# Layer 1 of a two-layer generator: four modulation rows summed on VectorE, and attention's maxima taken one unit ahead

## The chip, the cores and the metric

The kernel runs on one core of one Trainium2 chip. The metric is the device time of one execution in microseconds. The time before is 958.49 us, the median of three runs (957.53 to 961.4). All data are fp32; PE is TensorE, DVE VectorE, ACT ScalarE, POOL GpSimd, SP the engine whose queue issues the weight loads.

## The reference, cut to what matters

Two layers act on 256 latent tokens and 256 context tokens of width 1024. Each layer has a mixer and a mixture of 32 experts, each behind a norm and a modulation by a vector of the sample. Layer 1's mixer is an attention with two kinds of heads.

```python
mod_l = (silu(c) @ mod_w[i] + mod_b[i]).reshape(b, 6, 1, d)      # six rows of 1024 per layer
hl = modulate(rms_norm(xl, norm_g[i, 0]), mod_l[:, 0], mod_l[:, 1])
# layer 1: q, k, v from hl @ w_in, normed by head, rotated (rope) for latent tokens
s = einsum(q, k) * scale ; p = softmax(s) ; o = p @ v
o_m = attend(q_m, k_m, v_m, MLA_SCALE)                             # 4 heads
o_d = rms_norm(attend(q1, k1, v_d) - lam * attend(q2, k2, v_d), g_sub) * (1 - lam_init)   # 4 heads, two maps each
xl = xl + mod_l[:, 2] * (concat(o_m, o_d) @ w_out)
h2 = modulate(rms_norm(xl, norm_g[i, 1]), mod_l[:, 3], mod_l[:, 4])
xl = xl + mod_l[:, 5] * moe(h2)                                    # 32 experts in 8 groups, top 2 of one group
```

Layer 1 gives no context output, so rows 2 to 5 of its modulation are needed for the latent stream alone.

## The kernel before, in words

Every engine has its own program, and semaphores tie them. The order of work is written out by hand.

**Weights.** `stream_plan` lists all weight units in the order of their use, mostly 2 MB each. SP's loop (L970) issues them in that order, and each issue waits until the unit's slot is free. `slot_plan` (L154 on) gives the slots: a ring of 7, and for the experts four more places lent by other tensors (WORK_SLOT, X_SLOT, B_SLOT, PART_SLOT). WORK_SLOT of layer 1 waits for the 16th turned attention output, X_SLOT for the saved x and the routing's logits, PART_SLOT for the stored h2 rows. `freed` says which semaphore frees a unit: a modulation unit is freed by PE's multiplication of that row.

**Modulation.** A row of the modulation is 1024 x 1024 weights in two units. `mod_multiply(i)` runs 32 PE records with 32-column weights of the activated conditioning vectors (`mod_part`, L1029), ScalarE copies the bank (`mod_copy`, L1497), `mod_turn` turns it by four small matmuls (L1051), VectorE adds the bias (`mod_columns`, L1855). Rows 8 and 9 (row 2 and 3 of layer 1) are done during the projection, row 8 behind item 16 and row 9 behind the last item; rows 10 and 11 are cut into eight parts, one behind each of the units 8 to 15 of attention (`mod_in_attention`).

**Projection** (`project_pe`, the item loops of `attention_scalar` and `attention_vector`). 28 items of one tile of tokens each: 0 to 5 ckv and ql, 6 to 15 the 512-wide kd, qd and vd (11 and 13 to 15 are vd, without norm), 16 to 23 kvm, 24 to 27 qm. For each, PE multiplies (L473, L483, L486), ScalarE squares (L641, L638), VectorE sums the squares (`sums`, L1719), GpSimd takes the power -1/2 (L2203, L2204), VectorE scales the rows (`rows_of`, L1744, L1748, L1754) and rotates those of latent tokens (L1700 to L1706), PE turns them two items later (L504), ScalarE copies the columns.

**Attention.** 16 units: 0 to 7 are MLA heads, scored in pairs (L532, L535), 8 to 15 differential heads with two maps (L541). PE's step i holds scores(i), values(i-2) (L561), turn_o(i-3) (L571), a modulation part, and probs(i-1), the transposes of the probabilities (L550). ScalarE's step holds the squares of the output (L671), exps(i) (L656), o_cols(i-3) (L664) and the copy of the turned probabilities (L677). VectorE's step holds maxima(i) (L1791, L1793), output_rows(i-2) (L1819) and normalize(i) (L1800 to L1805). Bank 5 holds one unit's values at a time, so values(i) wait for output_rows(i-1). Afterwards come `project_out` (L1133), the norm and routing of the experts, and the experts (L1255, L1280).

Of the kernel before, what the change touches and what calls it, by code (L numbers as in the profile page):

```python
# [20 lines left out]
P = 128  # L21
D = 1024
# [131 lines left out]
def slot_plan(stream):  # L154
# [35 lines left out]

OIN = {"ckv": (768, 960), "ql": (0, 256), "kd": (960, 1472), "qd": (256, 768), "vd": (1472, 1984)}


def generator_kernel(nc, a, out):
# [4 lines left out]
    with ExitStack() as ctx:  # L199
# [135 lines left out]
        MOD_ITEM = 16  # L335
        MOD_BANK = (6, 6, 6, 6, 6, 6, 7, 6, 6, 6, 7, 7)
# [118 lines left out]
        def project_pe(pe, loaded, mod_multiply, mod_turn):  # L455
# [63 lines left out]
        def attention_pe(pe, mod_turn, mod_in_attention, gates):  # L519
# [44 lines left out]
            def turn_o(i):  # L564
                pe.wait_ge(sem("o_rows"), i + 1)
                if i:
                    pe.wait_ge(sem("o_cols"), i)
                else:

                    pe.wait_ge(sem("mod_rows"), 10)  # L570
                pe.transpose(bank[6][:, 0:P], OR[i % 2], ident).then_inc(sem("o_turned"), 1)  # L571

            for i in range(n_units + 3):
# [6 lines left out]
                if i == 2:  # L580
                    mod_turn(9)
                if 8 <= i < 16:
                    mod_in_attention(i - 8)
                if 0 <= i - 1 < n_units:
                    probs(i - 1)
                if i == n_units:
                    pe.wait_ge(sem("exp_done"), n_units - 1)
                    gates("a1", 1, 2, (1,), (0, 1))
                elif i == n_units + 1:
                    mod_turn(10)  # L590

        def attention_scalar(act, mod_copy, gate_rows):
# [26 lines left out]
            for i, (kind, t, p) in enumerate(ITEMS):  # L619
                if i == MOD_ITEM + 1:  # L620
                    mod_copy(8)
# [25 lines left out]
            mod_copy(9)  # L647
# [18 lines left out]
            def o_squares(i):  # L666
# [4 lines left out]
                act.activation(OR[j], bank[5][:, 0:P], ACT.Square, accum_out=oss[:, j:j + 1]).then_inc(sem("o_squares"), 1)  # L671
# [7 lines left out]
            for i in range(n_units + 3):  # L679
                if 0 <= i - 2 < n_units and UNITS[i - 2][0]:  # L680
                    o_squares(i - 2)
                if i == 12:
                    mod_copy(10)
# [6 lines left out]
                if i == n_units:  # L690
                    mod_copy(11)
                elif i == n_units + 1:
# [304 lines left out]
        def _(pe):  # L997
# [34 lines left out]
            def mod_in_attention(j):  # L1032

                i, part = 10 + j // 4, j % 4
                if part % 2 == 0:
                    loaded(pe, where[("mod",) + MOD_PAIRS[i] + (part // 2,)])
                if part == 0:
                    pe.wait_ge(sem("mod_cols"), 10)
                    pe.wait_ge(sem("mod_rows"), i)
                mm = mod_part(i, MOD_BANK[i], (2 * part, 2 * part + 1))  # L1040
                if part == 3:
                    mm.then_inc(sem("mod_mm"), 1)

            def mod_turn(i):

                pe.wait_ge(sem("mod_rows"), 12 if i >= 10 else i + 1)
# [7 lines left out]
            def mod(i):  # L1054
                mod_multiply(i)
                mod_turn(i)

# [78 lines left out]
            def route(L):  # L1136
# [61 lines left out]
                pe.wait_ge(sem("mod_cols"), (7, 12)[L])  # L1198
# [254 lines left out]
            project_pe(pe, loaded, mod_multiply, mod_turn)  # L1453
            attention_pe(pe, mod_turn, mod_in_attention, gates)
            mod_turn(11)
# [3 lines left out]
            pe.wait_ge(sem("mod_cols"), 12)  # L1459
# [8 lines left out]
        def _(act):  # L1468
# [203 lines left out]
            attention_scalar(act, mod_copy, gate_rows)  # L1672
# [700 lines left out]
```

## Time and profile before

| | us |
|---|---|
| median of 3 runs | 958.49 (957.53 to 961.4) |
| span of the profiled execution | 954.8 |
| PE busy | 851.6 (89%) |
| DVE busy | 323.4 (34%) |
| ACT busy | 170.0 (18%) |
| POOL busy | 170.5 (18%) |
| HBM read | 293.66 MB, 321 GB/s over the span |

The profile gives the profiled execution by its span, from the first to the last instruction; a time of its own around that isn't shown. The stages by the clock of the span: layer 0 to about 480 us, the norm of layer 1's mixer to 497, projection to 617.8, attention to 688.2, output projection to 715.8, norm and routing to about 731, experts to the end. Busy time of an engine is the sum of its instructions; a busy PE isn't a PE at its peak. The granted clock is 1.00 at 2.4 GHz and 0.50 at 1.2 GHz.

### The profile page before, as it was taken

What the parts mean: (1) busy time and instruction counts of PE and PEld (TensorE: products, weight loads), DVE (VectorE), ACT (ScalarE), POOL (GpSimd) and SP (SyncE); (2) the same over time, 40 slices, a digit from 0 to 9 for tenths busy, and PEclk for the clock granted to TensorE, in tenths of its full rate; (3) what the DMA queues carried; (4) which work ended last, traced back from release to release, by engine and by line L of the source; (5) the groups of instructions that cost most, each with busy time, mean ns of one, the idle gap of its engine ahead of it and who ended that gap; (6) DMA issues with size and microseconds to landing.
All of it is one profiled execution on the core that took longest, in us unless ns stands there. A gap on an engine that the chain in (4) does not pass through costs nothing.

```text
span 954.8 us, 10284 instructions
## 1 busy us (share of the span) xinstructions
PE 851.6 (89%) x3887; PEld 376.0 (39%) x3887; DVE 323.4 (34%) x711; ACT 170.0 (18%) x419; POOL 170.5 (18%) x210
## 2 busy tenths in 40 slices
PE   4899999999999999868769999888899999779786
PEld 2444445447333333223257443354546333223222
DVE  1279997217111211111132441636405111011011
ACT  2301022115000000000042112445414000000000
POOL 2100391221220222220212211300110111011001
PEclk9899999999999999889969999999999999889898
DMA  9999454709999999999989024372657999999994
GB/s 362 408 414 388 152 211 186 300 35 324 328 407 405 372 400 375 420 400 417 374 361 387 1 100 165 135 307 107 281 230 265 381 406 409 418 418 425 413 418 180
DMA packets 33975, 298.00 MB, mean 312 GB/s; under 512 B 6560, under 2 KB 6866, under 8 KB 16252
## 3 DMA queue, kind: packets, MB, share of 16 engines
q1 hardware_dynamic: 26928, 283.26, 73.5%
q0 software_dynamic: 6912, 13.92, 4.1%
q8 instruction: 39, 0.64, 0.3%
q14 instruction: 20, 0.16, 0.1%
q10 hardware_dynamic: 76, 0.02, 0.0%
HBM read 293.66 MB, written 12.58 MB: 321 GB/s over the span
## 4 chain that ended last, share of the span: by engine, by line
PE 50%; DMA 21%; DVE 15%; issue 6%; ACT 3%; SPq 3%; PEld 2%; POOL 0%; another core or an unknown queue 0%; PEldq 0%; POOLq 0%; DVEq 0%
PE bank L1255 14%; DVE WORK L2156 9%; PE bank L473 9%; PE bank L1280 7%; DMA ring<-in_gu_pack 5%; PE bank L1405 5%; DMA B<-in_gu_pack 5%; DMA WORK<-in_gu_pack 4%; DMA ring<-in_win_pack 3%; PE bank L1133 3%; SPq L970 2%; PE bank L1352 2%; DVE small L1791 1%; PE bank L1029 1%; DMA h_rows<-B 1%
## 5 line engine op out<-in xcount | busy, mean ns | idle before, releaser
L1255 PE MATMUL bank<-ring,hT 128*64 128x512 f32 x688 | 210.5, 633 | 23.4 <-DMA ring<-in_gu_pack 16.6
L2070 DVE SCALAR_TENSOR_TENSOR hT<-hT,WORK,bank 128x256 f32<-128x256 f32 x34 | 16.3, 480 | 327.3 <-ACT hT L1556 327.3
L1255 PEld LDWEIGHTS bank<-ring,hT 128*64 128x64 f32 x688 | 62.1, 145 | 117.9 <-issue 117.7
L2156 DVE SCALAR_TENSOR_TENSOR WORK<-WORK,par 128x512 f32<-128x512 f32 x116 | 90.7, 861 | 0.0
L473 PE MATMUL bank<-ring,hT 128*128 128x512 f32 (+2 forms) x256 | 88.0, 499 | 0.7 <-ACT hT L1519 0.7
L1280 PE MATMUL bank<-ring,WORK 128*64 128x512 f32 x368 | 83.5, 595 | 1.6 <-ACT WORK L1561 1.6
L1255 PE MATMUL bank<-WORK,hT 128*64 128x512 f32 x128 | 59.8, 609 | 9.1 <-issue 7.6
L1561 ACT ACTIVATE WORK<-bank 128x256 f32<-128x256 f32 x34 | 13.1, 384 | 281.9 <-PE bank L1264 281.9
L1352 PE MATMUL bank<-hT,ring 128*128 128x512 f32 x128 | 58.4, 616 | 2.2 <-DMA ring<-in_win_pack 2.2
L473 PEld LDWEIGHTS bank<-ring,hT 128*128 128x128 f32 x256 | 46.0, 190 | 35.8 <-issue 34.0
L1029 PE MATMUL bank<-ring,cs 128*32 128x512 f32 x384 | 49.2, 638 | 9.5 <-DMA ring<-in_mod_pack 7.4
L1255 PE MATMUL bank<-X,hT 128*64 128x512 f32 x112 | 53.9, 629 | 4.0 <-DMA B<-in_gu_pack 2.7
L1405 PE MATMUL bank<-ring,B 128*128 128x512 f32 x128 | 56.6, 596 | 0.8 <-DVE B L2173 0.8
L852 POOL DMA_INDIRECT hT<-h_rows,smalli x21 | 20.0, 954 | 170.8 <-PE bank L1229 87.8
L2203 POOL TENSOR_SCALAR small<-small 128x1 f32<-128x1 f32 (+2 forms) x46 | 11.4, 247 | 209.7 <-ACT WORK L671 66.3
L1255 PE MATMUL bank<-B,hT 128*64 128x512 f32 x96 | 45.3, 617 | 1.3 <-issue 1.3
L1280 PEld LDWEIGHTS bank<-ring,WORK 128*64 128x64 f32 x368 | 25.7, 137 | 48.2 <-issue 44.7
L1352 PEld LDWEIGHTS bank<-hT,ring 128*128 128x128 f32 x128 | 24.9, 198 | 34.2 <-issue 30.9
L1405 PEld LDWEIGHTS bank<-ring,B 128*128 128x128 f32 x128 | 23.8, 190 | 31.2 <-issue 27.7
L865 POOL DMA_INDIRECT latents<-WORK,smalli x8 | 8.2, 1029 | 153.4 <-DVE WORK L2088 130.5
L2204 POOL TENSOR_TENSOR small<-small,cst 128x1 f32<-128x1 f32 (+2 forms) x46 | 33.8, 734 | 3.8
L1556 ACT ACTIVATE hT<-bank 128x256 f32<-128x256 f32 x34 | 13.1, 384 | 118.6 <-PE bank L1255 114.7
(297 smaller groups left out, 1039.1 us busy)
## 6 DMA issues: line engine op xcount, KB each, us to landing
ring<-in_gu_pack SPq DMA_DIRECT2D x38, 2048.0 KB, 22.3
ring<-in_mod_pack SPq DMA_DIRECT2D x24, 2048.0 KB, 12.8
ring<-in_down_pack SPq DMA_DIRECT2D x20, 2048.0 KB, 26.7
WORK<-in_gu_pack SPq DMA_DIRECT2D x6, 2048.0 KB, 32.7
ring<-in_wout_pack SPq DMA_DIRECT2D x4, 2048.0 KB, 15.7
ring<-in_gu_pack SPq DMA_DIRECT2D x8, 1024.0 KB, 28.0
ring<-in_win_pack SPq DMA_DIRECT2D x3, 2048.0 KB, 36.8
X<-in_gu_pack SPq DMA_DIRECT2D x3, 2048.0 KB, 30.3
```

The source lines that it names most:

```text
L473: mm = pe.matmul(dst[:, 0:hi - lo], hT[:, k, t * P:(t + 1) * P], w[:, k, :], start=k == 0, stop=k == KC - 1)
L852: return pool.indirect_dma_start(XG[s], None, h2d[:, :], bass.IndirectOffsetOnAxis(ap=smalli[0:ST, i:i + 1], axis=0), bounds_check=rows_ - ...
L970: sp.dma_start(dst, src).then_inc(sem(f"weights_in{at}"), 16)
L1029: mm = pe.matmul(bank[b][at:at + 32, :], cs[:, k, :], w, start=k < 2, stop=k >= KC - 2)
L1133: mm = pe.matmul(bank[OUT_BANKS[L][i % 2]][:, :], lhs(k, j), w[:, k, :], start=k == 0, stop=k == KC - 1)
L1255: mm = pe.matmul(dst[ST * x:ST * x + ST, :], HG[L][s][:, k, :], columns(units[x], 512 * k, 512), start=k == 0, stop=k == KC - 1)
L1280: mm = pe.matmul(bank[5 + s][ST * h:ST * h + ST, :], HET[s][:, f, ST * x:ST * x + ST], columns(n, 2048 * x + 1024 * f + 512 * h, 512), sta ...
L1352: mm = pe.matmul(b[:, :], w[:, k, 256 * part + P * (m % 2):256 * part + P * (m % 2) + P], hT[:, k, :], start=k == 0, stop=k == KC - 1)
L1405: mm = pe.matmul(bank[OUT_BANKS[0][i % 3]][:, :], mixT[:, (k + 4) % KC, j * P:(j + 1) * P], w[:, (k + 4) % KC, :], start=k == 0, stop=k == ...
L2070: dve.scalar_tensor_tensor(out=T1[L][s], in0=SG[L][s], scalar=cwt[:, at:at + 1], in1=src[:, 0:DE], op0=ALU.mult, op1=ALU.mult).then_inc(se ...
L2156: ins = dve.scalar_tensor_tensor(out=acc, in0=src, scalar=w, in1=acc, op0=ALU.mult, op1=ALU.add)
L2204: pool.tensor_tensor(dst, dst, C("half", 0, 1).to_broadcast([P, n]), ALU.pow).then_inc(sem(name), 1)
```

## The change

It has two parts. First, rows 2 to 5 of layer 1's modulation are no longer multiplied on PE. VectorE accumulates, for the latent stream alone, weight rows times the conditioning value of each partition, over the eight chunks of the contraction, in 64 instructions of 128x512. They stand behind the items 6 to 15 of its projection program in the numbers of `SUM_STEPS`. PE then sums over the partitions: `sum_rows` for row 2 (as a row broadcast to all partitions), `sum_columns` for rows 3 to 5 (as columns). GpSimd clears the accumulator of row 2 and loads its bias. A modulation unit is freed by VectorE's count, and the order in which free slots are given is sorted by `LATER`. Second, in attention the maxima of unit i+1 are taken before unit i is normalised, and the first map of a differential unit isn't scaled: the second is weighed by lambda and the ratio of the sums, and 1/sum goes into the output rows and their squares. The cut diff (`gates`, `mod_copy`, `mod_turn` calls of these rows go away throughout):

```diff
 def slot_plan(stream):
+    where_second = stream.index(("lora",))
+    def order(at):
+        u = stream[held[at]]
+        if u in early:
+            return 0, early.index(u)
+        if u in LATER:
+            return 2, LATER.index(u)
+        return 1, held[at]
     for n, u in enumerate(stream):
         expert = u[0] in ("gu", "down")
+        if n > where_second and (not expert or WORK_SLOT not in free):
+            free.sort(key=order)
...
+LATER = [("mod", 1, 1, 0), ("mod", 1, 1, 1), ("oin", "ckv"), ("oin", "ql"), ("mod", 1, 2, 0), ("mod", 1, 2, 1), ("oin", "qd"),
+         ("mod", 1, 3, 0), ("mod", 1, 3, 1), ("oin", "kd"), ("mod", 1, 4, 0), ("mod", 1, 4, 1), ("mod", 1, 5, 0), ("oin", "vd"), ("mod", 1, 5, 1),
+         ("lora",), ("wout", 1, 0), ("wout", 1, 1)]
...
+        SUMMED = [(1, 2), (1, 3), (1, 4), (1, 5)]
+        SUMS = [[MR[:, h, :] for h in (0, 1)], [B[:, 2048 + 512 * h:2560 + 512 * h] for h in (0, 1)],
+                [B[:, 3072 + 512 * h:3584 + 512 * h] for h in (0, 1)], [GB[:, 0, 512 * h:512 * h + 512] for h in (0, 1)]]
+        SUM_STEPS = {6: 4, 7: 4, 8: 8, 9: 5, 10: 5, 11: 10, 12: 5, 13: 8, 14: 8, 15: 7}
         def freed(n):
             u = STREAM[n]
+            if u[0] == "mod" and u[1:3] in SUMMED:
+                return "sum_done", 4 * TAPS + 2 * KC * SUMMED.index(u[1:3]) + KC * (u[3] + 1)
...
         def project_pe(...):
             for i in range(len(ITEMS) + 2):
                 if i < len(ITEMS):
                     source(i)
-                if i == MOD_ITEM:
-                    mod_multiply(8)
-                elif i == MOD_ITEM + 4:
-                    mod_turn(8)
-                elif i == len(ITEMS):
-                    mod_multiply(9)
+                if i == len(ITEMS):
+                    sum_columns()
                 if i >= 2:
                     turn(i - 2)
         def attention_pe(...):
             for i in range(n_units + 3):
...
-                if i == 2:
-                    mod_turn(9)
-                if 8 <= i < 16:
-                    mod_in_attention(i - 8)
                 if 0 <= i - 1 < n_units:
                     probs(i - 1)
                 if i == n_units:
                     pe.wait_ge(sem("exp_done"), n_units - 1)
-                    gates("a1", 1, 2, (1,), (0, 1))
+                    sum_rows()
...
+            def sum_columns():
+                pe.wait_ge(sem("mod_cols"), 8)
+                for j in (1, 2, 3):
+                    pe.wait_ge(sem("sum_done"), 4 * TAPS + 2 * KC * (j + 1))
+                    for k in range(KC):
+                        mm = pe.matmul(bank[7][:, 16 * j + 2 * k:16 * j + 2 * k + 2], SUMS[j][k // 4][:, P * (k % 4):P * (k % 4) + P],
+                                       C("ones").to_broadcast([P, 2]), start=True, stop=True)
+                mm.then_inc(sem("mod_turned"), 1)
+            def sum_rows():
+                pe.wait_ge(sem("sum_done"), 4 * TAPS + 2 * KC)
+                for h in range(2):
+                    pe.matmul(bank[h][:, :], C("ones").to_broadcast([P, P]), SUMS[0][h], start=True, stop=True).then_inc(sem("gate_mms"), 1)
...
         def attention_vector(...):
+            def mod_sum(n):
+                j, k, h = n // (2 * KC), n // 2 % KC, n % 2
+                unit = where[("mod",) + SUMMED[j] + (k // 4,)]
+                if n == 0:
+                    dve.wait_ge(sem("brow_in"), 80)
+                if n % KC == 0:
+                    loaded(dve, unit)
+                if n >= 2:
+                    dve.wait_ge(sem("sum_done"), 4 * TAPS + n - 1)
+                w, c, acc = columns(unit, 1024 * (k % 4) + 512 * h, 512), cs[:, k, 1:2], SUMS[j][h]
+                if k == 0 and j:
+                    ins = ts(acc, w, c, None, ALU.mult)
+                else:
+                    ins = dve.scalar_tensor_tensor(out=acc, in0=w, scalar=c, in1=acc, op0=ALU.mult, op1=ALU.add)
+                ins.then_inc(sem("sum_done"), 1)
             for i, (kind, t, p) in enumerate(ITEMS):
...               # sums(i) and rows_of as before
+                for _ in range(SUM_STEPS.get(i, 0)):
+                    mod_sum(summed)
+                    summed += 1
...
             def normalize(i):
                 ins = dve.reciprocal(ri[:, u:u + 1 + d], es[:, o:o + 1 + d])
                 if d:
                     link(ins)
-                    tt(ri[:, u + 1:u + 2], ri[:, u + 1:u + 2], lam[:, 5:6], ALU.mult)
-                    link(ts(EX[:, i % 2, 0, :], EX[:, i % 2, 0, :], ri[:, u:u + 1], None, ALU.mult))
+                    link(dve.scalar_tensor_tensor(out=ri[:, u + 1:u + 2], in0=ri[:, u + 1:u + 2], scalar=lam[:, 5:6],
+                                                  in1=es[:, o:o + 1], op0=ALU.mult, op1=ALU.mult))
             def output_rows(i):
                 if UNITS[i][0]:
                     dve.wait_ge(sem("o_rstd"), i - 7)
-                    scale = ors[:, i % 2:i % 2 + 1]
+                    ins = ts(OR[i % 2], bank[5][:, 0:P], scale, ors[:, i % 2:i % 2 + 1], ALU.mult, ALU.mult)
...
+            maxima(0)
             for i in range(n_units + 2):
-                if i < n_units:
-                    maxima(i)
+                if i + 1 < n_units:
+                    maxima(i + 1)
                 if i >= 2:
                     output_rows(i - 2)
                 if i < n_units:
                     normalize(i)
...
         # GpSimd, behind the norm powers of layer 1's mixer
+            pool.wait_ge(sem("mod_turned"), 8)
+            link(pool.memset(MR[:, :, :], 0.0))
+            pool.dma_start(MR[0:1, :, :].rearrange("p a d -> p (a d)"), a["mod_b"][1:2, 2 * D:3 * D]).then_inc(sem("brow_in"), 16)
```

## Rows read from the trace of the kernel before

**Rows 1.** Table of windows: span, busy us (instructions) by engine, granted clock, DMA share, GB/s
```profile
747.00:920.00 173.00, 148.85 (x680) 50.29 (x680) 24.23 (x45) 9.60 (x25) 18.06 (x18) 0.94 1.01 414
```

**Rows 2.** SP's queue in order of time: start, us, engine, line, operation
```profile
687.52 0.33 SPq L970 DMA_DIRECT2D WORK<-in_gu_pack  x1
...
739.52 0.33 SPq L970 DMA_DIRECT2D B<-in_down_pack  x1
```

**Rows 3.** VectorE in order of time, conv taps
```profile
98.12 0.48 DVE L2154 TENSOR_SCALAR WORK<-WORK,par 128x512 f32<-128x512 f32 x1
98.52 19.29 DVE L2156 SCALAR_TENSOR_TENSOR WORK<-WORK,par 128x512 f32<-128x512 f32 x29
...
121.95 32.85 DVE L2156 SCALAR_TENSOR_TENSOR WORK<-WORK,par 128x512 f32<-128x512 f32 x29
```

**Rows 4.** VectorE in order of time, items 6, 10, 16 and 17 of the projection
```profile
526.40 0.69 DVE L1754 TENSOR_TENSOR WORK<-WORK,brow 128x512 f32<-128x512 f32 x1
...
551.66 0.69 DVE L1719 TENSOR_REDUCE small<-WORK 128x8 f32<-128x512 f32 x1 [0.97 <-ACT WORK L641]
554.45 0.69 DVE L1748 TENSOR_TENSOR WORK<-bank,small 128x512 f32<-128x512 f32 x1 [2.10 <-POOL small L2204]
...
555.90 0.69 DVE L1700 TENSOR_TENSOR WORK<-WORK,cst 128x512 f32<-128x512 f32 x1
...
557.57 0.42 DVE L1706 TENSOR_TENSOR WORK<-WORK 128x256 f32<-128x256 f32 x1
...
588.67 0.42 DVE L1719 TENSOR_REDUCE small<-WORK 128x2 f32<-128x256 f32 x1 [16.06 <-ACT WORK L638]
...
593.89 0.42 DVE L1744 TENSOR_TENSOR WORK<-bank,small 128x256 f32<-128x256 f32 x1
```

**Rows 5.** PE in order of time, end of the projection and start of attention
```profile
587.87 3.64 PE L1029 MATMUL bank<-ring,cs 128*32 128x512 f32 x32
...
616.01 0.88 PE L504 MATMUL bank<-cst,WORK 128*128 128x128 f32 x6
617.83 1.98 PE L532 MATMUL bank<-hT,WORK 128*128 128x512 f32 x4 [0.94 <-ACT WORK L613]
...
627.20 0.95 PE L1051 MATMUL bank<-cst,MR 128*128 128x4 f32 x8
```

**Rows 6.** PE in order of time, attention, to the output projection
```profile
637.79 1.88 PE L532 MATMUL bank<-hT,WORK 128*128 128x512 f32 x4
...
644.80 1.13 PE L541 MATMUL bank<-B,WORK 64*128 64x512 f32 x4
645.86 1.16 PE L561 MATMUL bank<-hT,WORK 128*128 128x128 f32 x8
...
648.05 0.66 PE L550 MATMUL bank<-cst,GB 128*128 128x128 f32 x4
648.63 1.13 PE L541 MATMUL bank<-B,WORK 64*128 64x512 f32 x4
...
674.83 1.13 PE L541 MATMUL bank<-B,WORK 64*128 64x512 f32 x4
...
688.22 27.71 PE L1133 MATMUL bank<-ring,B 128*128 128x512 f32 x64
```

**Rows 7.** VectorE in order of time, a differential unit
```profile
650.44 1.28 DVE L1791 TENSOR_REDUCE small<-bank 128x1 f32<-128x512 f32 x2
...
651.87 0.35 DVE L1819 TENSOR_SCALAR WORK<-bank,small 128x128 f32<-128x128 f32 x1
...
654.90 1.28 DVE L1791 TENSOR_REDUCE small<-bank 128x1 f32<-128x512 f32 x2
```

**Rows 8.** Table of windows around an idle stretch of PE among the experts
```profile
820.00:824.00 4.00, 0.52 (x4) 0.00 (x0) 0.00 (x0) 0.00 (x0) 0.00 (x0) 0.96 1.03 387
824.00:828.00 4.00, 2.70 (x8) 0.96 (x10) 0.00 (x0) 0.00 (x0) 0.00 (x0) 0.50 1.00 422
828.00:832.00 4.00, 4.00 (x16) 1.25 (x14) 0.00 (x0) 0.06 (x1) 0.00 (x0) 0.68 1.01 430
```

More of the change, by code:

```diff
@@ L453, in generator_kernel, with project_pe @@
         BLOCKS = {"kd": 4, "qd": 4, "ckv": 1, "ql": 2, "qm": 3, "kvm": 3}
-        def project_pe(pe, loaded, mod_multiply, mod_turn):
+        def project_pe(pe, loaded, sum_columns):
             def source(i):
@@ L1030, in mod_part @@
                 return mm
[L1032 to L1042, printed above, removed]
             def mod_turn(i):
-                pe.wait_ge(sem("mod_rows"), 12 if i >= 10 else i + 1)
+                pe.wait_ge(sem("mod_rows"), i + 1)
                 if i:
@@ L1671, in _ @@
             hcols("a1", 1)
-            attention_scalar(act, mod_copy, gate_rows)
+            attention_scalar(act, gate_rows)
             square_rows("m1", (0,))
@@ L1681, in _, with attention_vector @@
             moe_scalar(act, 1, moe_gate_rows, hcols, experts)
-        def attention_vector(dve, link, mod_columns):
+        def attention_vector(dve, link, loaded, sum_columns):
             tt, ts, red = dve.tensor_tensor, dve.tensor_scalar, dve.tensor_reduce
@@ L1765, in rows_of @@
                     dve.sem_inc(sem("rows_done"), 1)
-            waiting = None
-            for i, (kind, t, p) in enumerate(ITEMS):
-                if kind == "vd":
-                    continue
-                sums(i)
-                if waiting is not None:
-                    rows_of(waiting)
-                    waiting = None
-                if kind in ("kd", "qd"):
-                    rows_of(i)
-                else:
-                    waiting = i
+            def mod_sum(n):
[13 more added lines that the diff above has]
+                ins.then_inc(sem("sum_done"), 1)
+            waiting, summed = None, 0
+            for i, (kind, t, p) in enumerate(ITEMS):
+                if kind != "vd":
+                    sums(i)
+                    if waiting is not None:
+                        rows_of(waiting)
+                        waiting = None
+                    if kind in ("kd", "qd"):
+                        rows_of(i)
+                    else:
+                        waiting = i
+                for _ in range(SUM_STEPS.get(i, 0)):
+                    mod_sum(summed)
+                    summed += 1
             rows_of(waiting)
@@ L1856, in mod_columns, with sum_columns @@
                    par[:, r:r + 8].rearrange("p (h c) -> p h c", h=2).unsqueeze(3).to_broadcast([P, 2, 4, 2]), ALU.add).then_inc(sem("mod_cols"), 1)
+            def sum_columns():
+                r = R_MODB + 48 + 8 * 3
+                dve.wait_ge(sem("mod_turned"), 9)
+                tt(mods[:, 1, 3:6, :, :].rearrange("p v k s -> p (v k) s"), bank[7][:, 16:64].rearrange("p (k s) -> p k s", s=2),
+                   par[:, r:r + 24].unsqueeze(2).to_broadcast([P, 24, 2]), ALU.add).then_inc(sem("mod_cols"), 1)
             def norm_scale(L, n):
-                dve.wait_ge(sem("mod_cols"), 6 * L + (2 if n == 0 else 5))
+                dve.wait_ge(sem("mod_cols"), (2, 5, 8, 9)[2 * L + n])
                 g = par[:, R_NORM + 16 * L + 8 * n:R_NORM + 16 * L + 8 * n + 8]
@@ L2183, in _ @@
             norm_rows("a1")
-            attention_vector(dve, link, mod_columns)
-            mod_columns(10)
-            mod_columns(11)
+            attention_vector(dve, link, loaded, sum_columns)
             norm_scale(1, 1)
```

54 lines of the change are left out of this document (21 added, 33 removed).

## The prediction

> **What bounds the kernel now.** I read the table of windows first, then the DMA queue's own timeline, then PE and VectorE in order of time around the change. From 747 us to 920 us the 16 DMA engines are full, at 414 GB/s, and PE is busy only 149 of 173 us [rows 1]: layer 1's experts are bound by their weight stream. The question is what starts that stream. SP issues an expert unit only when its slot is free. WORK_SLOT waits for the last turned attention output and is issued at 687.52; PART_SLOT waits for the stored h2 rows and is issued at 739.52 [rows 2] (its first of four pieces). From there on the same 38 units have to come, whatever was loaded before. So the end is the time at which attention, output projection and routing are done, plus a constant. A microsecond more or less in front of 688 us comes out at the end; loads that land earlier while all slots are taken bring nothing.
>
> In front of it lies projection (497 to 617.83), which runs at PE's pace up to 587 us with the VectorE mostly idle, and attention (617.83 to 688.22) [rows 5, 6]. In the second half of attention each unit takes 4.46 us: VectorE's maxima start at 650.44 and again at 654.90 [rows 7]. It is a ring of maxima (1.43 us), ScalarE's two exponentials (about 1.6 with both hand-overs) and normalising (1.46).
>
> **Part 1, the modulation sums on VectorE.** Added: 64 instructions of 128x512 between item 6 and item 16: 58 multiply-and-adds, 6 multiplies. The conv taps are the same operation: 29 in 19.29 us, 0.663 each. The multiply costs 0.40 (98.12 to 98.52) [rows 3]. Sum: 58 x 0.663 + 6 x 0.40 = 40.9 us. The tap row of 120 us, beside long GpSimd operations, gives 1.13 each [rows 3]; here GpSimd has only its small powers, and these run while VectorE waits for them, so I take 0.663.
>
> Does VectorE have room? An item with rope runs from its sum at 551.66 to 557.57 + 0.35 = 557.9, so 6.26 us, of which 2.1 are a wait for GpSimd's power between 551.66 + 0.69 and 554.45 [rows 4]. That wait can't take the new work: sums, power and rows follow each other in program order, and the steps stand behind them. An item without rope lacks 555.90 to 557.9: 4.2 us. Walk: item 6 ends at 526.40 + 0.63 = 527.0 [rows 4]; between there and item 16 stand four rope items (7, 9, 10, 12) and one without (8): 4 x 6.26 + 4.2 = 29.2 us. With 40.9 us of steps that is 70.1, plus 0.3 idle before item 7 arrives: VectorE reaches item 16's sums at 597.4 instead of 588.67 [rows 4], 8.8 us late. The windows of PE's items (7.3 us) would have fitted steps and busy time; they don't fit the five waits for the power. The loads are in time: each unit has at least 4 us between the freeing of its slot and its first use, and one 2 MB unit takes 2.1 MB / 414 GB/s = 5 us only where more time is there.
>
> What that costs PE: nothing up to item 15 (item 12's turn is wanted at 579.6 and VectorE's walk has its rows done at 579.5). Then PE stands at the turn of item 16. Before, the rows of item 16 began at 593.89 [rows 4], since PE ran the 32 matmuls of modulation 8 first (from 587.87, 3.57 us [rows 5]). Now they begin 1.8 us (two sums of 0.6, and the rest of the power) behind 597.4: 599.2, so 5.3 us late. That is the 8.8 less the 3.5 which the removed matmuls give back. The later items keep their pace, a ring through ScalarE, GpSimd and VectorE; the removed turn lies in PE's slack. Term: **+5.3**.
>
> PE is then idle from 589.7 to 599.6. After an idle stretch of about 5 us (PE busy 0.52 of 820 to 824, and idle into the next window) the granted clock, 0.96, went to 0.50 and was back on the way to 1.00 (0.68) once PE was busy again for some 5 us [rows 8]: 1.2 GHz, then 2.4. A pair of items is 2.4 us of PE work in a ring of 3.46; at half clock 4.9. Over 5 to 9 us that is 1.5 to 2.7 us: term **+2.0**.
>
> Where modulation 9's multiplication stood (3.57 us before the last turns at 616.01 [rows 5]), PE now sums 24 columns. A turn of four such matmuls with a 128x128 weight is 0.81 to 0.95 us [rows 5], 0.2 each: 4.9 us. Bounds: 1.2 us (0.05 each, if only the columns counted) to 5.7. I take 4.9: it is the same form. The last turns come 1.3 later, while VectorE's last rows end within 0.2 of 616.01: term **+1.3**, from -0.2 to +2.1.
>
> Mod columns, copies and parts 10 and 11 leave attention. The parts (about 1.06 us each, one beside each unit from 8 on) lay in PE's slack: the 4.46 of [rows 7] does not change with them. Only modulation 9's turn, behind unit 2's values, was on the path: -0.7. The two row sums (4 records of 0.43) replace sixteen gate records of 0.11: 0. The added memset and 4 KB DMA stand on GpSimd behind the last norm power at 491 and before its first power at 501: 0; if late they'd only hold the first step, wanted at 527.
>
> **Part 2, maxima one unit ahead, first map unscaled.** Removed: one scaling pass on VectorE and its link, 0.48 us; the small product becomes a linked one, so normalising falls from 1.46 to 1.07. The maxima leave the ring of VectorE and ScalarE. What is late next is found in PE's order, which is unchanged: scores(i), values(i-2), turn(i-3), probs(i-1). VectorE's is now maxima(i+1), rows(i-2), normalise(i). So maxima(i+1) need scores(i+1), which PE issues behind probs(i-1), which need normalise(i-1): everything VectorE does in a step waits for PE, and values(i-2) wait for bank 5, that is for rows(i-3), which now stand behind maxima(i). The ring for a differential unit: scores to maxima 1.17 (1.13 and hand-over), maxima 1.43, output rows 0.35 + 0.06, values 1.0, turn 0.11, probabilities 0.58 to the next scores [rows 6, 7]: 4.70 us. Through normalising instead: 1.17 + 1.43 + 0.27 + 1.07 + 0.07 + 0.58 = 4.6. Before, the scores of unit 8 to those of unit 15 took 674.83 - 644.80 = 30.0 us [rows 6]; now 7 x 4.70 = 32.9: **+2.9**. At the end the rings run out much as before: +0.4.
>
> In the first half a pair took 644.80 - 637.79 = 7.0 us [rows 6], with values starting right behind the scores (2.9 us). Now they wait for maxima (0.84) and output rows (0.41) behind the scores: +1.3 for each pair once the pipe is full, twice: **+2.6**, less the 0.7 of above. Attention: 2.9 + 0.4 + 2.6 - 0.7 = **+5.2**.
>
> **Sum.** 5.3 + 2.0 + 1.3 + 5.2 = +13.8 us. The profiled execution's span is 954.8, and the median of the runs, 958.49, lies 3.7 above it; nothing of that edge is touched. Span 968.6, time 972.3. The order of slots changes, but the number of units left at the routing doesn't: 0.
>
> **Rivals.**
> A. Maxima ahead works as meant (other side): the two engines overlap and a unit falls to what its busiest engine holds, about 3.1 us on VectorE (1.43 + 0.27 + 1.07 and hand-overs). Then 8 x (4.46 - 3.1) = -11 in attention, and with projection's +8.6 not quite eaten: 956; with the sums hidden too (modulation 8's 3.5 us gained, 1.3 lost) -2.2 - 11: 945. It decides at the point where scores(i+1) are issued before normalise(i-1) is done; the order of PE's queue speaks against it, the free time of all engines in attention for it. Chance 0.11.
> B. Only one of the two losses arrives: steps shorter than taps, or slack in the ring that I don't see: +4.8 to +9, 963 to 967. Chance 0.14.
> C. Nothing arrives: the weight stream absorbs it. For it speaks that the stream is the bound for 200 us; against it that its start is tied to the slots [rows 2]. 958.5. Chance 0.08.
> D. The clock. In a differential unit PE would be busy 2.8 of 4.7 us. If the granted clock falls to half as in [rows 8], scores, values and probabilities double, 2.7 us a unit; over half of the eight units +11: 983.
> The Trainium skill's page "TensorE: Matmul & The Clock Gate" (section "Why this matters for your kernels") warns of idle gaps between bursts that return the array to 1.2 GHz. The rows agree for a gap of about 5 us; whether many gaps of 1 us do it no row shows. Chance of D 0.07.
> E. The change doesn't do what it says: the first step waits for the mod_b row and all sums slide. Even 5 us more would only add to the +5.3. Inside the range, no chance of its own.
>
> **Numbers.** Forecast 0.60, its own range 966 to 979 (each of the four terms off by a third, and the column sum's bounds). B 0.14, A 0.11, C 0.08, D 0.07. The range 961 to 983 leaves out A, C and a part of D. A difference of 0.5% (4.8 us) is about what can be told from none. Slower: 0.60 + 0.07 + 0.12 of B = 0.79; same: C and the rest of B, 0.10; faster 0.11.
>
> **What would show it.** Steps: VectorE's multiply-and-adds at 0.66 us, the last of them near 597, PE idle between 590 and 599, clock 0.5 behind. Columns: 48 short PE records over 4.9 us. Attention: VectorE idle about 1.8 us before each maxima, waiting for PE's scores; units of 4.7 us; pairs of 8.2. Scores of unit 0 near 626, output projection near 702, DMA full from 753 on. Wrong if: VectorE is through with its steps at 589; units fall under 4.46; or the end moves less than the start of the output projection.

## The result, and the profile after

The changed kernel takes 989.87 us (median of 4 runs, 988.5 to 995.5) against 958.47: a ratio of 1.033 (1.030 to 1.036), 31 us slower. 972.3 was forecast, with a range of 961 to 983. The span of the profiled execution went from 954.8 to 988.2 us, +33.4. By stages, each from its first PE row:

| stage | before | after | difference | forecast |
|---|---|---|---|---|
| up to the projection | 497.35 | 500.76 | +3.4 | 0 |
| projection, to the first scores | 120.5 | 129.3 | +8.8 | +8.6 |
| attention, to the output projection | 70.4 | 90.9 | +20.5 | +5.2 |
| from there to the end | 266.6 | 267.3 | +0.7 | 0 |

VectorE in order of time, kernel after (start, us, line, operation, idle time before and its releaser), answering to [rows 4] and [rows 7]:

```profile
591.36 9.36 DVE L1788 SCALAR_TENSOR_TENSOR GB<-ring,cs,GB 128x512 f32<-128x512 f32 x14
600.63 0.41 DVE L1724 TENSOR_REDUCE small<-WORK 128x2 f32<-128x256 f32 x1
...
602.47 0.42 DVE L1749 TENSOR_TENSOR WORK<-bank,small 128x256 f32<-128x256 f32 x1 [0.58 <-POOL small L2235]
...
668.33 1.29 DVE L1816 TENSOR_REDUCE small<-bank 128x1 f32<-128x512 f32 x2 [2.86 <-PE bank L558]
...
669.76 0.35 DVE L1844 TENSOR_SCALAR WORK<-bank,small 128x128 f32<-128x128 f32 x1
```

A step takes 0.67 us (9.36 / 14) as forecast, and item 16's sums begin at 600.63, which is 597.2 on the clock of before: 597.4 was forecast. Its rows begin at 602.47. In attention VectorE stands idle for 2.86 us, waiting for PE's scores (L558), before it takes the maxima (1.8 us were forecast); then come the output rows (L1844), for which PE's values wait.

PE in order of time, kernel after, answering to [rows 5] and [rows 6]:

```profile
500.76 1.54 PE L494 MATMUL bank<-ring,hT 128*128 128x192 f32 x8 [0.68 <-ACT hT L1524]
...
603.24 0.87 PE L525 MATMUL bank<-cst,WORK 128*128 128x128 f32 x3 [10.17 <-DVE WORK L1750]
...
622.15 3.63 PE L1054 MATMUL bank<-cst,B 128*128 128x2 f32 x32
625.64 2.29 PE L1054 MATMUL bank<-cst,GB 128*128 128x2 f32 x16
627.79 1.52 PE L525 MATMUL bank<-cst,WORK 128*128 128x128 f32 x6
630.04 3.78 PE L549 MATMUL bank<-hT,WORK 128*128 128x512 f32 x4 [0.73 <-ACT WORK L621]
...
662.44 1.13 PE L558 MATMUL bank<-B,WORK 64*128 64x512 f32 x4
665.55 1.13 PE L578 MATMUL bank<-hT,WORK 128*128 128x128 f32 x8 [1.98 <-DVE WORK L1844]
...
667.15 1.13 PE L558 MATMUL bank<-B,WORK 64*128 64x512 f32 x4
...
672.24 2.08 PE L558 MATMUL bank<-B,WORK 64*128 64x512 f32 x4
...
703.57 2.08 PE L558 MATMUL bank<-B,WORK 64*128 64x512 f32 x4
...
720.93 5.42 PE L1139 MATMUL bank<-ring,B 128*128 128x512 f32 x12 [0.46 <-ACT B L669]
```

The first differential unit is 4.71 us long (662.44 to 667.15), 4.70 being the forecast. From the third unit's scores (672.24) on the same four matmuls take anything from 1.13 to 2.08 us, and from the second unit on the distance to the next is 5.1 to 7.1 us. The first pair's scores take 3.78 where [rows 5] have 1.98. Half the clock is what doubles them, as the table of windows shows (columns as in [rows 1]; the granted clock is the number behind POOL):

```profile
600.00:610.00 10.00, 6.05 (x19) 3.34 (x20) 5.87 (x20) 4.54 (x14) 4.49 (x10) 0.67 0.99 420
...
630.00:640.00 10.00, 7.98 (x15) 3.12 (x16) 1.76 (x5) 2.15 (x5) 0.00 (x0) 0.67 0.00 0
...
660.00:670.00 10.00, 5.61 (x36) 3.54 (x34) 3.49 (x10) 4.61 (x12) 0.00 (x0) 1.00 0.01 2
670.00:680.00 10.00, 7.76 (x32) 5.42 (x34) 3.95 (x11) 3.79 (x12) 0.75 (x2) 0.57 0.00 0
680.00:690.00 10.00, 5.78 (x29) 3.40 (x26) 5.83 (x14) 3.37 (x12) 0.75 (x2) 0.84 0.00 0
...
700.00:710.00 10.00, 6.24 (x29) 4.40 (x30) 5.05 (x13) 3.13 (x11) 0.78 (x3) 0.78 0.00 1
```

Most of the miss lies in attention: 15.3 of the 19.6 us by which the span exceeds the forecast. (A ring is a circle of waits through several engines that comes round once per unit.) The theory to test: the rings are as forecast, but behind the gaps that they leave in PE, and behind the column sums before them, the granted clock falls to half. Its rivals: the rings themselves are longer than worked out, or the clock is a consequence of the 10 us in which PE waited at item 16.

### The profile page after: what moved, and what is told of

The parts are those of the page before. It is cut to its first block, busy times and chain, and to the rows that moved or that the text cites. A ratio compares the mean times of both kernels' runs of the same rounds, so it can differ in the third digit from the quotient of the medians.

```text
span 988.2 us, 10096 instructions
## 1 busy us (share of the span) xinstructions
PE 856.6 (87%) x3763; PEld 384.3 (39%) x3763; DVE 361.2 (37%) x764; ACT 169.1 (17%) x415; POOL 172.5 (17%) x212
## 4 chain that ended last, share of the span: by engine, by line
PE 44%; DMA 20%; DVE 19%; issue 6%; SPq 4%; ACT 3%; POOL 2%; PEld 1%; another core or an unknown queue 0%; PEldq 0%; DVEq 0%; POOLq 0%
PE bank L1261 13%; DMA ring<-in_gu_pack 11%; DVE WORK L2189 9%; PE bank L1286 6%; PE bank L1411 5%; PE bank L494 3%; DMA ring<-in_win_pack 3%; SPq L972 3%; PE bank L1139 3%; DMA ring<-in_down_pack 3%; PE bank L578 2%; DVE B L1788 2%; PE bank L1358 2%; DVE small L1816 1%; PE bank L558 1%
## 5 line engine op out<-in xcount | busy, mean ns | idle before, releaser
L1031 PE MATMUL bank<-ring,cs 128*32 128x512 f32 x256 | 33.9, 666 | 9.0 <-DMA ring<-in_mod_pack 7.8
```

The lines of the kernel that those rows point to most:

```text
L1031: mm = pe.matmul(bank[b][at:at + 32, :], cs[:, k, :], w, start=k < 2, stop=k >= KC - 2)
```

## The experiments

Each ratio is to runs of the kernel before made beside that experiment: 956.58 us for e1 to e4, 958.11 for e5, e8, f1 and f2, 958.54 for f3, f4, e9 and g1. "After" is the changed kernel, +31.4 us against its own before. Stages are read from one profiled execution each.

**e1, gaps of attention filled.** After, with throwaway matmuls (their results are never read) behind the scores and no other edit:

```diff
                 if 0 <= i - 3:
                     turn_o(i - 3)
+                if i == 2:
+                    pe.wait_ge(sem("mod_cols"), 9)
+                if 2 <= i < n_units:
+                    for _ in range(1 if i < 8 and i % 2 else 2):
+                        n = 256 if i < 8 and i % 2 else 384
+                        pe.matmul(bank[7][:, 0:n], ident, cst[:, 0:n], start=True, stop=True)
```

> The changed kernel with PE kept busy while it waits for VectorE in attention: two throwaway matmuls of 128x384 (1.3 us at the full clock) behind the scores of each step, one of 128x256 in the odd steps of the first half; nothing is left out. Theory (the clock): the changed kernel's attention is 90.9 us long (630.0 to 720.9) where the rings alone give about 76, since PE is thin and is granted half the clock in much of it; with the fillers the clock stays at 1.00, differential units fall from 6 to 7 us to about 4.7, attention to 75 to 78, the time from 989.9 to about 976. Rival (the rings are longer by themselves, the clock only follows): attention stays at 88 or more, time 987 to 992. Second rival (the fillers stand in the way): attention grows, over 992.

Measured: 981.92 us, ratio 1.026 (1.024 to 1.028). PE and the windows of e1:

```profile
666.62 1.13 PE L558 MATMUL bank<-B,WORK 64*128 64x512 f32 x4
...
695.44 1.13 PE L558 MATMUL bank<-B,WORK 64*128 64x512 f32 x4
```

```profile
630.00:640.00 10.00, 8.02 (x19) 2.57 (x17) 1.76 (x5) 2.16 (x5) 0.00 (x0) 0.70 0.00 0
...
670.00:680.00 10.00, 8.88 (x48) 5.29 (x47) 6.14 (x15) 4.10 (x14) 0.75 (x2) 1.00 0.00 0
```

Six units between these scores make 28.8 us, 4.80 each, and the clock is 1.00 in every window from 640 to 700. Attention falls from 90.9 to 83.4 us although PE has more to do. The rings are as worked out; the 5.1 to 7.1 us of after were the clock. Attention is still 5 us longer than the upper end of what was expected, and 7.8 longer than the prediction's 75.6. Of these 7.8 us 4.8 lie ahead of the first differential unit's scores (661.91), where the clock was 0.50 to 0.75 from 625 to 640, which e1 hardly fills. Another 2.4 lie behind the last unit's scores, with 0.83 from 700 to 710; no run fills that tail.

**e3, maxima back in their own step.** Everything else as after:

```diff
-            maxima(0)
             for i in range(n_units + 2):
-                if i + 1 < n_units:
-                    maxima(i + 1)
+                if i < n_units:
+                    maxima(i)
```

> The changed kernel with the maxima of a unit back in its own step, as before the change; sums on VectorE and the unscaled first map stay. Theory (the order of maxima makes the ring longer, and the longer ring makes PE thin): differential units 4.1 us, attention 66 to 70 us instead of 90.9, clock near 1.00, time 966 to 970. Rival (taking the modulation parts out of attention thins PE by itself): the granted clock still falls in the second half, attention 75 to 82, time 974 to 981.

Measured: 968.79 us, ratio 1.014 (1.011 to 1.017): +12 us where after has +31. Attention takes 71.5, 19.4 less than after and a little over the 66 to 70 expected. PE, and a window of e3:

```profile
664.09 1.13 PE L558 MATMUL bank<-B,WORK 64*128 64x512 f32 x4
...
668.21 1.13 PE L558 MATMUL bank<-B,WORK 64*128 64x512 f32 x4
```

```profile
670.00:680.00 10.00, 6.46 (x42) 4.47 (x43) 7.47 (x18) 5.96 (x19) 1.49 (x4) 1.00 0.00 0
```

A unit is 4.12 us, and the clock is 1.00 from 635 to 690, though the modulation parts are gone from this stage too. What holds the 4.12 us is the circle of maxima, exponentials and normalising, one behind the other. VectorE's maxima follow its normalising without a gap (a row without brackets had no wait), and ScalarE's exponentials wait for them:

```profile
671.16 1.28 DVE L1816 TENSOR_REDUCE small<-bank 128x1 f32<-128x512 f32 x2
672.70 0.69 ACT L661 ACTIVATE GB<-bank,small 128x512 f32<-128x512 f32 x1 [0.33 <-DVE small L1818]
```

About three-fifths of the loss of after (19 of 31 us) hang on the order of the maxima.

**e4, the maxima alone.** Before, with the maxima taken ahead by the same lines, and nothing else.

> The kernel before with one edit: maxima one unit ahead. Modulation stays on PE, its parts in attention too, and both maps are scaled. Theory (the ring through scores, maxima, output rows, values and probabilities): here the modulation part of 1.06 us stands in the ring as well, so a differential unit takes about 5.8 us at the full clock against 4.3 before, pairs 8.2 against 6.9: attention about 84 instead of 70.4, time about 972, and the granted clock stays near 1.00 since PE is busy 3.7 of 5.8 us. Rival A of the prediction (maxima ahead works): attention under 70, time under 958. If the clock falls as in the changed kernel: attention over 90, time over 978.

Measured: 980.29 us, ratio 1.025 (1.022 to 1.028). PE of e4:

```profile
658.46 1.06 PE L1029 MATMUL bank<-ring,cs 128*32 128x512 f32 x8
...
660.05 1.13 PE L541 MATMUL bank<-B,WORK 64*128 64x512 f32 x4
663.15 1.55 PE L561 MATMUL bank<-X,WORK 128*128 128x128 f32 x8 [1.98 <-DVE WORK L1819]
...
664.85 1.94 PE L1029 MATMUL bank<-ring,cs 128*32 128x512 f32 x8
...
667.47 1.13 PE L541 MATMUL bank<-B,WORK 64*128 64x512 f32 x4
```

The units here are 5.86 us at full clock, several 7.4: the ring of 4.70 plus the modulation part of 1.06, which stands between values and probabilities and so lies on the ring. Attention is 90.3. From unit 8's scores to unit 15's it is 46.8 us instead of 30.0: seven units of 5.86 would be 41.0, so the longer ring gives 11 us and the clock (0.83 in three of four windows from 660 to 700) some 6. Order and clock do this without any sum on VectorE, and without a matmul taken away.

**e5, scores ahead too.** Rival A of the prediction named its point of decision: scores(i+1) issued before normalise(i-1) is done. e5 is after, with PE's queue changed to that:

```diff
+            scores(0)
             for i in range(n_units + 3):
-                if i < n_units:
-                    scores(i)
+                if i + 1 < n_units:
+                    scores(i + 1)
```

> Kernel after, with PE's scores one unit ahead too (scores(0) before the loop, scores(i+1) in step i). Theory: the maxima ahead lengthen the unit only because PE issues scores(i+1) behind probs(i-1), so VectorE's whole step waits for PE. With the scores issued ahead that wait is gone: VectorE's idle time before the maxima falls from 1.8 us to under 0.5, a differential unit takes 3.3 to 4.0 us (VectorE holds 1.43 + 0.27 + 1.07 us of it and hand-overs), PE is busy 2.8 of it and the granted clock stays at 1.00 from the third unit on; attention 66 to 73 us against 90.9 in after, and the time is 964 to 971. Rival 1: the unit stays at 4.7 us, because bank 5 and the output rows close another ring; then 988 as in after. Rival 2: only the clock was the loss, and a differential unit takes 4.7 us at clock 1.00: 977.

Measured: 965.56 us, ratio 1.009 (1.005 to 1.012), +7.5 us where after has +31; attention 66.2. PE, then ScalarE:

```profile
657.92 1.13 PE L558 MATMUL bank<-B,WORK 64*128 64x512 f32 x4
...
660.61 1.13 PE L558 MATMUL bank<-B,WORK 64*128 64x512 f32 x4
...
664.72 1.13 PE L558 MATMUL bank<-B,WORK 64*128 64x512 f32 x4 [1.34 <-ACT GB L662]
...
668.82 1.13 PE L558 MATMUL bank<-B,WORK 64*128 64x512 f32 x4 [1.34 <-ACT GB L662]
```

```profile
671.08 0.37 ACT L678 ACTIVATE WORK<-bank,small 128x128 f32<-128x128 f32 x1 [1.56 <-PE bank L578]
671.43 0.68 ACT L662 ACTIVATE GB<-bank,small 128x512 f32<-128x512 f32 x1
```

Units begin at 2.69 us, PE without a gap, and become 4.10 once the outputs of a differential unit have to be squared. ScalarE's squares (L678) wait 1.56 us for PE's values (L578). The two exponentials (L662) stand behind the squares, PE's next scores wait 1.34 us for the exponentials, and the next values stand behind these scores: squares 0.35, exponentials 1.5, scores and values 2.2 with hand-overs, 4.1 in all. That ring is why A's 3.1 us was too low. GpSimd's power (L2236) makes VectorE's output rows wait 1.09 us at 672.58, but they are done at 672.99, before PE's values at 673.98 need them. The 4.12 us of e3 come from another ring, so that the two are alike is chance.

**e2, the overrun of VectorE.** After, with up to three of the steps of items 7 to 10 and 12 put between sums and rows, where VectorE waits for GpSimd's power:

```diff
                 if kind != "vd":
                     sums(i)
+                    if waiting is None:
+                        for _ in range(min(3, steps)):
+                            mod_sum(summed)
...                 # the rest of the item's steps behind its rows, as before
```

> The changed kernel with up to three of each item's modulation steps placed between the item's sum of squares and its rows, where VectorE waits 2.1 us for GpSimd's power (items 7, 8, 9, 10 and 12); same number of steps. Theory (it was the five waits that made VectorE late): 4 or 5 times 2.0 us come back, item 16 is summed at about 592 instead of 600.6, PE's wait of 10.2 us at its turn shrinks to under 2, projection from 129.3 to about 121, time about 981. Rival (40 us of steps are too much whatever their place): VectorE still 8 us late, time 988 to 991.

Measured: 984.40 us, ratio 1.030 (1.027 to 1.033). VectorE, then PE of e2:

```profile
529.33 0.69 DVE L1724 TENSOR_REDUCE small<-WORK 128x8 f32<-128x512 f32 x1 [0.21 <-ACT WORK L647]
529.93 2.07 DVE L1788 SCALAR_TENSOR_TENSOR MR<-ring,cs,MR 128x512 f32<-128x512 f32 x3
532.95 0.69 DVE L1753 TENSOR_TENSOR WORK<-bank,small 128x512 f32<-128x512 f32 x1 [0.94 <-POOL small L2241]
```

```profile
593.68 0.87 PE L525 MATMUL bank<-cst,WORK 128*128 128x128 f32 x3 [4.65 <-DVE WORK L1750]
...
612.99 4.70 PE L1054 MATMUL bank<-cst,B 128*128 128x2 f32 x32
617.55 3.55 PE L1054 MATMUL bank<-cst,GB 128*128 128x2 f32 x16
```

PE waits 4.65 us at item 16 instead of 10.17, so the overrun is what was said, though the wait is not under 2 as expected. The steps aren't free there: from sums to rows it is 3.6 us, not the 2.8 of [rows 4]. And the column block now takes 8.0 us instead of 5.6: projection falls by 2.8 us against after's 129.3, not by 8. That 129.3 is itself the lowest of four: with the same code up to the scores, e1, e3 and e5 have 131.2, 132.0 and 131.8. All four reach item 16's turn 102.5 us behind the start; they differ in the ring and the block behind it, where the clock stands differently. Against those three e2 saves about 5 us.

**g1 and f1, gap or block?** g1 fills the wait at item 16 with 22 throwaway matmuls; f1 takes the block apart, three columns behind each of eight turns, and leaves the wait. First g1's edit, then f1's:

```diff
+                if i == 18:
+                    pe.wait_ge(sem("mod_cols"), 8)
+                    for _ in range(22):
+                        pe.matmul(bank[6][:, 0:384], ident, cst[:, 0:384], start=True, stop=True)
```

```diff
-                if i == len(ITEMS):
-                    sum_columns()
                 if i >= 2:
                     turn(i - 2)
+                if 19 <= i < 27:
+                    sum_columns(i - 19)
```

> Kernel after with 22 throwaway matmuls of PE (128x384, 0.39 us each, 8.5 us in all) in the 10.2 us in which PE waits at item 16's turn. Theory: that idle time puts the clock to half; after it 10 to 15 us run at half clock before the block of column sums begins. Filled, the clock is 1.00 up to the block, projection falls by 2 to 3.5 us (129.3 to 132 in the kernels with the gap, so to 127 to 129), the block still takes 3.6 to 8 us and still drops the clock behind it; attention stays near 90, time 985 to 987. Rival: the low clock at the start of attention comes from this gap and not from the block: then the block takes 2.3 us, the first pair 5.5 and the time is 978 to 982.

> Kernel after, with the 24 sums over partitions of the modulation not in one block before the last turns but in eight parts of three (6 of the 48 short records each) behind the turns of steps 19 to 26. Theory: the block of 48 two-column matmuls is seen as idle by the clock gate; spread between real matmuls it keeps 1.00, the first scores come 4 to 6 us earlier (the block took 5.6 us, the scores behind it 3.78 instead of 1.9), and attention's first pair is 5.5 us instead of 7.45. The halves of clock in the differential units stay (their gap is the same 2 us). Time 980 to 984 against 988 to 990 in after. Rival: the wait at item 16's turn, not the block, holds the clock low till the scores; then projection shortens by 1 to 2 us only and the first pair still takes 7 to 8 us: 987.

Measured: g1 992.04 us, ratio 1.035 (1.031 to 1.040); f1 997.37, ratio 1.040 (1.037 to 1.044). Windows and PE of g1:

```profile
600.00:610.00 10.00, 8.31 (x32) 4.22 (x31) 3.87 (x14) 4.97 (x16) 3.18 (x7) 1.00 0.86 369
...
625.00:630.00 5.00, 4.27 (x19) 3.83 (x19) 0.21 (x1) 1.28 (x4) 0.00 (x0) 0.50 0.31 128
```

```profile
620.59 3.63 PE L1058 MATMUL bank<-cst,B 128*128 128x2 f32 x32
624.08 3.27 PE L1058 MATMUL bank<-cst,GB 128*128 128x2 f32 x16
```

Window of f1:

```profile
600.00:625.00 25.00, 23.14 (x72) 16.03 (x73) 9.04 (x31) 8.84 (x27) 7.51 (x18) 0.52 0.44 186
```

In g1 the clock is 1.00 up to the block (1.00 also from 615 to 620, 0.94 from 620 to 625) and 0.50 behind it, and the first pair takes 8.02 us: the gap isn't needed for it. PE's short waits just ahead of the block are those of before (1.35 and 0.36 us), where the 32 records of modulation 9 (512 columns each) stood in its place and the clock stayed at 1.00. (The fillers took 14.35 us for the 10 to be filled and made the turn late by some 4; so g1 tells the cause, not a price.) f1 shows the other half, and my theory for f1 fell, its rival of 987 us too: behind the same gap the clock is back at 1.00 by 610 in after, while with the two-column matmuls among the real ones it is 0.52 over 25 us, with PE 23.1 of 25 us busy. Projection took 140.4.

**e8, the unscaled map alone.** Before, with only the first map left unscaled (`normalize`, `output_rows` and the squares' scale as in after).

> The kernel before with only the unscaled first map (one scaling pass on VectorE less in each differential unit, the factor taken into the square's scale and the output rows). Theory: the ring maxima, exponentials, normalise of the second half loses 0.39 us a unit, 4.46 to 4.1, eight times: attention 70.4 to 67.3, time 953 to 956. Rival: the unit is held by PE's queue, so nothing: 957 to 959; or a unit at 4.1 with PE less idle changes the clock: no.

Measured: 958.17 us, ratio 1.000 (0.998 to 1.002): no gain. Seven units together take 29.0 us instead of 30.0. The fastest units, 3.84 us in both kernels, are PE's own work with its modulation part, and there a shorter VectorE chain brings nothing. Attention in the profile is even 0.7 us longer, 71.1: behind the first pair, and behind the same PE program as in before with the same wait of 1.98 us, the clock was 0.68 from 620 to 625 where before has 1.00. So whether the clock falls there can differ between executions of one order, and a difference of 1 or 2 us in one profile may be that.

**f2, f3, f4, e9: what the parts are worth when put right.** f2 is after with up to four steps between, the columns spread and the maxima in step; f3 is f2 with maxima and scores ahead; f4 is f3 with nine throwaway matmuls between the last turns:

```diff
                 if 19 <= i < 27:
                     sum_columns(i - 19)
+                if i >= len(ITEMS) - 1:
+                    for _ in range((5, 2, 2)[i - len(ITEMS) + 1]):
+                        pe.matmul(bank[6][:, 0:384], ident, cst[:, 0:384], start=True, stop=True)
```

e9 is before with the unscaled map, maxima and scores ahead, and the modulation left on PE.

> The kernel after with all three losses taken away: up to four steps of items 7 to 10 and 12 between sums and rows, the column sums spread as in f1, and the maxima in the unit's own step as before; what is left of the change is the modulation sums on VectorE and the unscaled first map. Theory (sum of the single effects): projection 118 to 123 us (120.5 before), attention 65 to 68 (70.4 before, less 8 x 0.39 for the scaling pass, less modulation 9's turn), rest 267: span 948 to 955, time 951 to 959, same or slightly faster than before. Rival: the granted clock falls at the start of attention whatever stands there, attention 72 or more, time 963 to 968.

> f2 with maxima and scores both one unit ahead in place of the maxima in their own step. e5 took 66.2 us for attention against 90.9, f2 had projection at 119.9. If both effects add, span 119.9 + 66 + 267 on the common start: 952, time 951 to 955, faster than before by 3 to 7 us. Rival: shorter units thin PE enough that the clock falls again, attention 70 or more, time 957 to 962.

> f3 with nine throwaway matmuls of PE (128x384, 0.39 us each) in the idle time around the last turns: five, two and two. In f2 PE was idle 2.6, 1.2 and 0.7 us there, the granted clock was 0.67 to 0.69 from 615 to 630 and the first pair took 7.76 us; before, with modulation 9's 32 matmuls there, the clock was 1.00 and the pair 5.51. Theory: the idle time just ahead of attention costs the clock of the first two pairs; with the fillers it stays at 1.00 and attention loses another 2.5 to 4 us: time 948 to 951. Rival: the fillers delay the turns that they stand before and the clock falls in the pairs' own gaps: same as f3 or 1 us worse.

> The kernel before with only the unscaled first map, the maxima one unit ahead and PE's scores one unit ahead; modulation stays on PE as it was. Projection 120.5 as before, its matmuls of modulation 9 keep the clock at 1.00 into attention; a differential unit 2.7 to 4.1 as in e5 although PE has modulation parts 10 and 11 beside it: attention 62 to 67 against 71 to 73, time 949 to 953. Rival: parts 10 and 11 (1.06 us each) stand in a ring that has no slack left, 0.5 to 1 us a unit: attention 70, time 956 to 959.

| kernel | median us | ratio to before | projection | attention |
|---|---|---|---|---|
| f2 | 958.68 | 1.000 (0.998 to 1.002) | 119.9 | 71.1 |
| f3 | 954.76 | 0.996 (0.994 to 0.997) | 119.9 | 66.5 |
| f4 | 951.99 | 0.994 (0.991 to 0.996) | 120.3 | 64.5 |
| e9 | 957.44 | 0.999 (0.997 to 1.001) | 120.5 | 67.3 |

Windows around the last turns, f3, then f4:

```profile
615.00:620.00 5.00, 4.25 (x7) 1.67 (x7) 0.33 (x2) 0.64 (x2) 0.00 (x0) 0.50 0.40 167
```

```profile
610.00:615.00 5.00, 5.00 (x24) 3.38 (x24) 3.90 (x14) 1.66 (x5) 1.77 (x4) 1.00 0.36 85
615.00:620.00 5.00, 5.00 (x20) 3.01 (x19) 2.22 (x11) 1.28 (x4) 0.00 (x0) 1.00 0.80 334
```

PE of e9:

```profile
644.58 1.13 PE L541 MATMUL bank<-B,WORK 64*128 64x512 f32 x4
...
646.84 1.06 PE L1031 MATMUL bank<-ring,cs 128*32 128x512 f32 x8
...
648.42 1.13 PE L541 MATMUL bank<-B,WORK 64*128 64x512 f32 x4
```

f3 and f4 beat both kernels; f4 by 6.5 us against before (0.65%). f2 stays at the time of before: its attention, 71.1 for the 65 to 68 expected, has the clock at 0.67 from 615 to 630, with no column block there but PE idle 2.64 and 1.20 us at the last turns, and a first pair of 7.76 us. Between f3 and f4 the intervals overlap, though in the profiles attention is 2.0 us shorter and the clock there 1.00 instead of 0.50. e9's rival held in time (956 to 959), with attention between the two: the part of 1.06 us stands on PE's path, a unit of 2.69 becomes 3.84. f3, which has the sums on VectorE in its place, is 0.3% faster than e9. That is what the change's first half is good for, and in these runs only behind scores taken ahead; f2 with fillers was not run.

## Why the prediction was wrong, by its own steps

- **VectorE's overrun, +5.3: right.** On a common start of the projection, item 16's turn comes 5.2 us late (599.8 against 594.65), the same in e1, e3 and e5. e2 took its cause away and the wait halved.
- **Clock behind the gap +2.0 and columns +1.3: the sum right in one execution, by luck; the split not.** From item 16's turn to the last turns it is 24.55 us instead of 21.36 (616.01 less 594.65): +3.2. But the columns take 5.6 us, 2.1 more than the 3.57 of the modulation they replace, and 6.6 to 8.0 in g1, e1, e5, e3 and e2; so the ring at half clock cost about 1.1. The last turns to the scores add 0.4. In e1, e3 and e5 projection is +10.7 to +11.5 instead of +8.8, beyond even the upper ends of the two terms (2.7 and 2.1 with the 5.3). At the full clock 48 such records would be 5.4 us (an estimate, from the first 32 in 3.63 us), so 0.2 a column was a little low, and that the clock would fall while they run, as in g1, stood in no term.
- **Attention's rings, +5.2: right where the clock is 1.00.** 4.71 a unit in after and 4.80 in e1 for 4.70; a pair 8.18 for 8.2.
- **The step that failed is the term for attention, +5.2: it priced the longer rings at a granted clock of 1.00.** The fall of the clock stood in the sum at nothing; it was held apart as rival D, at 0.07, for half of the differential units alone (+11). It came, and further. Attention's +20.5 consists of: first scores to unit 8's scores +5.4 (1.9 forecast), the seven units +11.1 (2.9), the tail +4.0 (0.4): 15.3 us more than worked out. e1 gives back 7.5 of them by filling gaps alone, from unit 2 on, all of it in the differential units and the tail. That the rest is the clock too is argued from the clock of 0.50 to 0.83 in what e1 leaves long, and f4 against f3 shows 2.0 us of it at the first pair; the tail was not tested. e3, whose ring leaves PE idle 1.36 us of 4.12 instead of 1.98 of 4.71, brings attention to 71.5 at a clock of 1.00 in these units. The prediction had asked of [rows 8] only whether gaps of 1 us would do what a gap of 5 did, though it had itself worked out gaps of 2 us in every unit. Taking the eight parts of 1.06 us of modulation matmuls out of the stage wasn't enough for the fall: in e3 they are gone too. The Trainium skill's page "TensorE: Matmul & The Clock Gate", section "A second HAM failure mode: psum-queue depth-cycling", tells of a kernel whose array idles briefly between groups of matmuls and changes between both clocks; the windows from 670 to 710 (0.57, 0.84, 0.73, 0.78) agree, while e3 with its shorter gaps stays at 1.00. It was there to be weighed.
- **Start of the projection, +3.4: not forecast and still open.** The order of work up to there is unchanged, and the nine other kernels built on after start it at 496.6 to 499.0; no run tells what it was in this execution.
- **Rivals B and C** fell: both losses arrived, and the end moved with the start of the output projection (+32.7 there, +33.4 in all).
- **Rival A** was rightly held back for this change, since PE's order decides. With that order changed (e5) it came true in part: attention is 66.2 us against 70.4 before, 4.2 of its 11, at 4.1 us a unit instead of 3.1. Most of the 24 us between after and e5 is the loss undone, of which e3 gives back 19 without it.
- **"The 4.46 does not change with the parts"** was true of the waiting units only, and 4.46 is not the mean: the seven units took 4.29 each. 3.83 in [rows 6] (644.80 to 648.63) is PE's full queue, which e9 shows again.

## What to carry to other kernels

Taking work ahead on one engine helps only if its input is issued ahead too; otherwise everything queued behind it waits as well, and the ring grows. When a change lengthens a ring, work out PE's idle time per turn and price the stage at both levels of the clock: the same order with its gaps filled was 7.5 us shorter here (e1), and up to 15.3 us, more than any term of the sum, may be the clock's. Work moved to a half-idle engine must be laid into that engine's own waits, counted one by one, and not into its free share.

## What the runs showed of the hardware

- A PE that is busy by the records can stand at half clock: it went from 1.00 to 0.50 over a block of 48 two-column records with no wait over 1.35 us ahead of it (g1), and was 0.52 over 25 us in which such records stood among real ones, behind a gap of 10 us (f1). Where it was 1.00 before and PE had no long wait (f2, 597 to 612 us), it stayed at 1.00 with the same records spread out: 14.1 of 15 us busy.
- How busy PE is in a window doesn't tell the clock by itself: 6.46 of 10 us at 1.00 in e3, 7.76 at 0.57 in after. There the low clock itself makes PE busier: at 1.00 the same work would be about 4.4 us (an estimate, 7.76 x 0.57).
- GpSimd's power took longer beside VectorE's accumulations: 3.6 us from sums to rows instead of 2.8 (e2). Both of its instructions are longer there, up to 0.63 and 2.03 us instead of 0.20 and 1.64. Which of its accesses is delayed was not tried.
